# The samples' depthwise convolution moved from VectorE to GpSimd, and six prompt taps from TensorE to VectorE

## The reference

```python
def conv_mix(x, buf, w_pw1, b_pw1, w_dw, b_dw, ln_g, ln_b, w_pw2, b_pw2):
    h = x @ w_pw1 + b_pw1
    u = h[..., :D] * jax.nn.sigmoid(h[..., D:])
    full = jnp.concatenate([buf.astype(u.dtype), u], axis=1)      # 30 past rows, then the new ones
    c = depthwise_conv(full, w_dw, width=31) + b_dw               # one filter of 31 taps per channel
    cn = layernorm(c) * ln_g + ln_b
    out = jax.nn.silu(cn) @ w_pw2 + b_pw2
    return out, full[:, -30:]
...
def peer(x, w_q, sub_keys, u_tab, v_tab):                         # per token and head
    idx, gate = top 16 of the product keys, softmax
    act = gelu(sum_d u_tab[idx] * x)
    return sum_k gate_k * act_k * v_tab[idx_k]
```

## Time and profile before

| | |
|---|---|
| median of 3 runs | 3850.49 us (3847.3 to 3853.64) |
| the profiled execution's own time | 3850.32 us |
| its span, first to last instruction | 3848.5 us |
| mean granted clock of TensorE | 0.859 of full speed |
| busy: TensorE, VectorE, ScalarE, GpSimd | 74%, 71%, 38%, 37% of the span |
| gathers | 1152, with 1208 of 1313 MB moved |

### The profile page before, as it was taken

The page is one execution under the profiler, slowest core; times in us unless marked ns, Lnnn a source line. Parts: engine busy times, 40 slices in busy tenths (PEclk is TensorE's granted clock), DMA queues, the critical chain, the costliest instruction groups (busy, mean ns, idle before and its releaser), DMA issues.

```text
span 3848.5 us, 56215 instructions
## 1 busy us (share of the span) xinstructions
PE 2857.6 (74%) x20248; PEld 1343.3 (35%) x20248; DVE 2727.9 (71%) x6400; ACT 1449.0 (38%) x4376; POOL 1423.6 (37%) x1272
## 2 busy tenths in 40 slices
PE   7899998697666667788869657798786666666655
PEld 4667766442222212343324213344232222222211
DVE  5666665467666667777787767888776777777774
ACT  1333332134333334454444334444443333333333
POOL 0111111144444444444444444343344444444442
PEclk9999998897888878898889779999898877878777
DMA  2111110499999999999999999999999999999996
GB/s 79 36 31 27 43 31 18 159 426 426 427 426 426 427 427 426 418 388 402 408 426 422 426 425 426 389 383 373 397 416 426 426 425 427 427 426 426 425 426 283
DMA packets 230360, 1313.42 MB, mean 341 GB/s; under 512 B 58816, under 2 KB 62016, under 8 KB 82368
## 3 DMA queue, kind: packets, MB, share of 16 engines
q0 software_dynamic: 165888, 1208.03, 75.0%
q1 hardware_dynamic: 64192, 101.79, 7.5%
HBM read 1303.88 MB, written 5.86 MB: 340 GB/s over the span
## 4 chain that ended last, share of the span: by engine, by line
DMA 37%; PE 19%; DVE 18%; ACT 3%; issue 3%; DVEq 1%; ACTq 1%; POOL 1%; POOLq 0%
DMA arena<-in_uv,arena 37%; DVE arena L1780 9%; PE psum L1352 8%; PE psum L1314 4%; PE psum L1404 3%; PE psum L1434 2%; DVE arena L1869 1%; ACT wbuf L1570 1%; ACT arena L1565 1%; PE psum L1424 1%; DVE arena L1708 1%; POOL arena L1294 1%; DVE arena L1843 1%; DVE arena L1705 1%; DVE level L1732 0%
## 5 line engine op out<-in xcount | busy, mean ns | idle before, releaser
L1352 PE MATMUL psum<-arena,wbuf 64*64 64x512 f32 (+1 forms) x8704 | 1456.4, 743 | 864.5 <-ACT wbuf L1570 844.0
L1294 POOL DMA_INDIRECT arena<-in_uv,arena x1152 | 1344.2, 1167 | 1773.7 <-PE psum L1352 1571.7
L1780 DVE SCALAR_TENSOR_TENSOR arena<-arena 128x1024 f32<-128x1024 f32 x1152 | 1395.9, 1223 | 577.1 <-DMA arena<-in_uv,arena 550.4
L1352 PEld LDWEIGHTS psum<-arena,wbuf 64*64 64x64 f32 (+1 forms) x8704 | 336.1, 155 | 1759.9 <-ACT wbuf L1570 1364.1
L1561 ACT ACTIVATE arena<-arena 128x2 f32<-128x2 f32 x576 | 117.0, 203 | 1664.7 <-DVE arena L1780 1644.6
L1570 ACT ACTIVATE wbuf<-cst,arena 128x64 f32<-128x64 f32 x1152 | 338.1, 340 | 41.6 <-issue 2.4
L1314 PE MATMUL psum<-arena,wbuf 128*128 128x256 f32 (+1 forms) x1024 | 308.4, 449 | 8.4 <-DVE arena L1791 5.8
L1565 ACT ACTIVATE arena<-arena 128x1 f32<-128x1 f32 x1152 | 276.7, 287 | 41.5 <-issue 2.1
L1314 PEld LDWEIGHTS psum<-arena,wbuf 128*128 128x128 f32 x1024 | 201.6, 207 | 172.4 <-issue 130.7
L419 PE MATMUL psum<-arena,wbuf 128*128 128x288 f32 x672 | 189.0, 415 | 2.8 <-ACT arena L705 2.8
L1036 POOL COPY x<-arena 128x256 f32<-128x256 f32 x8 | 3.2, 397 | 423.2 <-DVE x L883 423.2
(11 more groups left out here) (273 smaller groups left out, 3155.4 us busy)
## 6 DMA issues: line engine op xcount, KB each, us to landing
wbuf<-in_w_q SPq DMA_DIRECT2D x64, 576.0 KB
arena<-in_w_pw SPq DMA_DIRECT2D x48, 512.0 KB
arena<-in_uv,arena POOLq DMA_INDIRECT x1152
wbuf<-in_w_rkv SPq DMA_DIRECT2D x24, 512.0 KB, 4.2
wbuf<-in_w_o SPq DMA_DIRECT2D x8, 512.0 KB, 3.7
arena<-in_w_o SPq DMA_DIRECT2D x8, 512.0 KB
x<-in_x SPq DMA_DIRECT2D x5, 576.0 KB, 6.1
arena<-in_state SPq DMA_DIRECT2D x16, 128.0 KB, 2.9
```

The source lines that it names most:

```text
L1294: pool.indirect_dma_start(ring[:, g % RING, :], None, I["uv"][p // 2], bass.IndirectOffsetOnAxis(ap=idx[:, s % 4, j:j + 1], axis=0)).then_ ...
L1352: last = pe.matmul(ps[e * HD:(e + 1) * HD, 2 * (u % 2) + a if u < NB else 4, :], diag[t, g % DIAGS, :], ring[t, g % RING, D + e * 512:D + ...
L1780: stt(out=row, in0=row, scalar=1.0, in1=tok[p % 2][:, UNITS[p % 2].index(u), :], op0=ALU.mult, op1=ALU.mult, accum_out=dots[:, g % COLS:g ...
```

## The change

The samples' convolution leaves VectorE and becomes a generator `samples` on GpSimd, run between its gathers. GpSimd's row is the one whose buffer its last gather took over, 11 rows behind that gather (`tick.now = g - RING - PHASE_ROW[2]`). VectorE's single reduction over 31 taps becomes additions in halves: 15 and 15, then 8, 4, 2, 1. Where one of these reads what the last one wrote, GpSimd waits for its own semaphore `sample_step`. `sampled` counts finished chunks; SP, VectorE and TensorE wait for it where they reuse or need what the samples' convolution reads or writes. In `cB` TensorE does 10 taps of the prompt and VectorE 21; `cA` stays at 16 and 15.

```diff
--- before.py
+++ after.py
@@ -1071,7 +1071,7 @@
 
 
     RING, DIAGS, LEAD, COLS = 11, 8, 2, 12
-    PE_TAPS = 16
+    PE_TAPS = (16, 10)
     HALFK = TOPK // 2
     UNITS, WIDTH, FROM = ((0, 1), (2, 3, 4)), (256, 320), (0, 256)
     PICKS = (TOPK, TOPK, TOPK, TOPK, HALFK)
@@ -1107,7 +1107,7 @@
     idx = R.cut(4, TOPK, dtype=U32)
     neg_max, gate, share, gate_sum, gate_inv = R.cut(4), R.cut(4, TOPK), R.cut(4, TOPK), R.cut(4), R.cut(4)
     dots, gelu, coef = R.cut(COLS), R.cut(COLS), R.cut(COLS)
-    tap_diags = R.cut(PE_TAPS, HD)
+    tap_diags = R.cut(max(PE_TAPS), HD)
     spare = R.cut(1)
     wb = [R.cut(C, P) for _ in range(2)]
     ups, uss = [R.cut(PAST + 2 * P) for _ in range(2)], [R.cut(SB, PAST + ST) for _ in range(2)]
@@ -1163,6 +1163,7 @@
             dve_names += [f"{n}.{x}{c}" for c in range(C) for x in ("glu", "tapped")]
             dve_names += each(n, "centred") + each(n, "scaled") + each(n, "into_x")
     pe_b, act_b, dve_b = Steps(K.sem("bg_pe"), pe_names), Steps(K.sem("bg_act"), act_names), Steps(K.sem("bg_dve"), dve_names)
+    sampled, sample_step = K.sem("conv_sampled"), K.sem("conv_sample_step")
     last_out = ("n0A", "n0B", "n1A", "n1B")
     ps = K.ps
     BANK = (5, 6)
@@ -1220,7 +1221,7 @@
                         sp.dma_start(wb[j], I["w_pw1"][2 * c + j]).then_inc(bl[j], 16)
                     if half:
                         if c >= 2:
-                            sp.wait_ge(dve_b.sem, dve_b.value(f"{n}.tapped{c - 2}"))
+                            sp.wait_ge(sampled, c - 1)
                             sp.wait_ge(stored, 32 * (c - 1))
                         sp.dma_start(uss[c % 2][:, :, 0:PAST], I["state_conv"][c]).then_inc(small[c % 2], 16)
                         if c:
@@ -1285,7 +1286,50 @@
 
         @block.gpsimd
         def _(pool):
+            tick = Tick()
+            HT = ST // 2
+
+            def samples(n, t):
+
+
+                summed = 0
+                for c in range(C):
+                    at = t["conv"] + c * t["chunk"] + 1
+                    us = uss[c % 2]
+                    weight = unsq(K.par[:, TAP0:TAP0 + TAPS, c], 1, SB)
+                    bias = K.par[:, B_DW, c:c + 1].unsqueeze(1).to_broadcast([P, HT, SB])
+                    yield from tick.until(at)
+                    pool.wait_ge(dve_b.sem, dve_b.value(f"{n}.glu{c}"))
+                    for e in range(2):
+                        out = cv[1][:, c, 2 * P:WIDTH[1]].rearrange("p (b t) -> p t b", t=ST)
+                        for i in range(HT):
+                            last = pool.tensor_tensor(prods[:, i], us[:, :, e * HT + i:e * HT + i + TAPS], weight, ALU.mult)
+                            if i < HT - 1:
+                                yield from tick.until(at + 4 * e + (i + 1) // 3)
+                        last.then_inc(sample_step, 1)
+                        summed += 1
+                        pool.wait_ge(sample_step, summed)
+                        for i in range(0, HT, 2):
+                            last = pool.tensor_tensor(prods[:, i:i + 2, :, 0:15], prods[:, i:i + 2, :, 0:15], prods[:, i:i + 2, :, 16:31], ALU.add)
+                        for m in (8, 4, 2, 1):
+                            last.then_inc(sample_step, 1)
+                            summed += 1
+                            yield from tick.until(at + 4 * e + (2 if m == 8 else 3))
+                            pool.wait_ge(sample_step, summed)
+                            last = pool.tensor_tensor(prods[:, :, :, 0:m], prods[:, :, :, 0:m], prods[:, :, :, m:2 * m], ALU.add)
+                        last.then_inc(sample_step, 1)
+                        summed += 1
+                        pool.wait_ge(sample_step, summed)
+                        last = pool.tensor_tensor(out[:, e * HT:(e + 1) * HT], prods[:, :, :, 0], bias, ALU.add)
+                        if e == 0:
+                            last.then_inc(sample_step, 1)
+                            summed += 1
+                            yield from tick.until(at + 4)
+                            pool.wait_ge(sample_step, summed)
+                    last.then_inc(sampled, 1)
+
             pool.memset(spare, 0.0).then_inc(row_done, RING)
+            work = samples("cB", times(2))
             for s, (p, head, u) in enumerate(SEQ):
                 pool.wait_ge(index_ready, s + 1)
                 for j in range(PICKS[u]):
@@ -1294,6 +1338,13 @@
                     pool.indirect_dma_start(ring[:, g % RING, :], None, I["uv"][p // 2],
                                             bass.IndirectOffsetOnAxis(ap=idx[:, s % 4, j:j + 1], axis=0)
                                             ).then_inc(here[g % RING], 16)
+                    if p == 2:
+                        tick.now = g - RING - PHASE_ROW[2]
+                        next(work, None)
+                if s + 1 == len(SEQ) or SEQ[s + 1][0] == 3:
+                    tick.now = 10 ** 6
+                    for _ in work:
+                        pass
 
         @block.tensor
         def _(pe):
@@ -1427,15 +1478,17 @@
                 def taps(c, at):
                     pe.wait_ge(act_b.sem, act_b.value(f"{n}.diags{c}"))
                     pe.wait_ge(dve_b.sem, dve_b.value(f"{n}.glu{c}"))
-                    for k in range(PE_TAPS):
+                    for k in range(PE_TAPS[half]):
                         yield from tick.until(at + k // 8)
                         for e in range(2):
                             q = slice(e * HD, e * HD + HD)
-                            last = pe.matmul(part[q], tap_diags[q, k, :], ups[c % 2][q, k:k + 2 * P], start=k == 0, stop=k == PE_TAPS - 1)
+                            last = pe.matmul(part[q], tap_diags[q, k, :], ups[c % 2][q, k:k + 2 * P], start=k == 0, stop=k == PE_TAPS[half] - 1)
                     last.then_inc(pe_b.at(f"{n}.tapped{c}"), 1)
 
                 def add_up(c):
                     pe.wait_ge(dve_b.sem, dve_b.value(f"{n}.tapped{c}"))
+                    if half:
+                        pe.wait_ge(sampled, c + 1)
                     return pe.matmul(total, K.ones, cv[half][:, c, :], start=c == 0, stop=c == C - 1)
 
                 yield from tick.until(t["project"])
@@ -1831,20 +1884,11 @@
                         dve.tensor_copy(up[:, 0:PAST], carry[:, c, :])
                         stt(out=up[:, PAST:], in0=ps[:, 5, 0:2 * P], in1=sg[:, 0:2 * P], **how)
                         dve.wait_ge(small[c % 2], 16 * (c // 2) + 16)
+                        if c >= 2:
+                            dve.wait_ge(sampled, c - 1)
                         stt(out=us[:, :, PAST:], in0=ps[:, 5, 2 * P:w].rearrange("p (b t) -> p b t", t=ST),
                             in1=sg[:, 2 * P:w].rearrange("p (b t) -> p b t", t=ST), **how).then_inc(dve_b.at(f"{n}.glu{c}"), 1)
                         dve.drain()
-
-                def sample_taps(c, us, e):
-
-                    weight = unsq(K.par[:, TAP0:TAP0 + TAPS, c], 1, SB)
-                    for i in range(ST // 2):
-                        at = e * (ST // 2) + i
-                        tt(prods[:, i], us[:, :, at:at + TAPS], weight, ALU.mult)
-                    dve.drain()
-                    out = cv[half][:, c, 2 * P:w].rearrange("p (b t) -> p t b", t=ST)[:, e * (ST // 2):(e + 1) * (ST // 2), :]
-                    dve.tensor_reduce(out=out, in_=prods, op=ALU.add, axis=AX.X)
-                    dve.drain()
 
                 if half == 0:
                     for up in ups:
@@ -1855,17 +1899,11 @@
                     yield from tick.until(at)
                     glu(c, up, us)
                     out = cv[half][:, c, 0:2 * P]
-                    if half:
-                        for e in range(2):
-                            yield from tick.until(at + 1 + 2 * e)
-                            sample_taps(c, us, e)
-                        rest = cv[half][:, c, 2 * P:w]
-                        ts(rest, rest, K.par[:, B_DW, c:c + 1], None, ALU.add)
                     yield from tick.until(at + 5)
                     dve.wait_ge(act_b.sem, act_b.value(f"{n}.tap_sum{c}"))
                     spread = t["chunk"] - 6
-                    for k in range(PE_TAPS, TAPS):
-                        yield from tick.until(at + 5 + (k - PE_TAPS) * spread // (TAPS - PE_TAPS))
+                    for k in range(PE_TAPS[half], TAPS):
+                        yield from tick.until(at + 5 + (k - PE_TAPS[half]) * spread // (TAPS - PE_TAPS[half]))
                         last = stt(out=out, in0=up[:, k:k + 2 * P], scalar=K.par[:, TAP0 + k, c:c + 1], in1=out, op0=ALU.mult, op1=ALU.add)
                         if k < TAPS - 1:
                             dve.drain()
```

## The result

The changed kernel takes 3899.3 us (3897.9 to 3901.2, 4 runs), the kernel before 3851.8 in the same comparison: a ratio of 1.0125, 95% interval 1.0111 to 1.0139. That is +47.5 us where 3870, some +20, was forecast. The sign was right, but the size was forecast at less than half. The time lies 0.7 us inside the upper end of the range (3838 to 3900), and that is luck: the range reached so far only for the rival in which GpSimd is the bound, which is not what happened.

What follows compares the result with a forecast made beforehand. VectorE was taken to bound the sample half's convolution, DMA close behind. From 3850.3 us, minus 32.6 net VectorE work, plus 47 collision, plus 5 late gathers, gives 3870 us; range 3838 to 3900.

Steps and rivals of the forecast that it cites:

- the rival in which GpSimd is the bound: Sample half's convolution: dear products and full waits make GpSimd need 360 to 384 us; 3885 to 3908 us, chance 0.15.
- The bound: Sample half's convolution, 325.8 us: VectorE, busy 289.5 us, is the tighter resource, with the DMA engines close behind.
- the DMA floor: Same stretch: even a free VectorE gains only about 7 us before the DMA engines bind, 31 at 426 GB/s.
- What is removed and added: VectorE in the convolution: 58.4 us of sample work removed, 25.8 us of prompt taps added, net 32.6 us less.
- So I leave it: VectorE's 11.4 us wait for the tap sum, left unchanged although VectorE arrives 7 us earlier in each chunk.
- GpSimd's own time: The 176 operations moved to GpSimd in the convolution take 98 us, between 80 and 128.
- The collision: Convolution: GpSimd's operations and VectorE's two-input SBUF instructions exclude each other, costing VectorE 47 us, ends 27 and 80.
- the 0.71: Share of VectorE's time in which dots and taps hold its two inputs, 207 of 293 us; scales the collision.
- The gathers behind it: Gathers queued behind GpSimd's products come late, mostly covered by the ring of 11 rows: 5 us for the stretch.
- The other waits: Waits for the gate product, SP's conv state load, sample reuse and TensorE's column sum were each put at 0.
- The faster rival: The two engines seldom meet in the convolution and the DMA engines bind: 3830 to 3843 us, chance 0.25.
- The signs named beforehand: Convolution of the changed kernel: expected instruction lengths, GpSimd's busy time, row waits and stretch length, all else as before.

Runs made afterwards that it cites:

- the taps alone: Kernel before with only TensorE's prompt taps cut to 10 and VectorE's raised to 21 in the sample half's convolution, samples still on VectorE: 3869.0 us, ratio 1.0048.
- 16 taps on TensorE: Changed kernel with the taps back at 16 on TensorE and 15 on VectorE, only the samples on GpSimd: 3878.6 us, ratio 1.0072.
- steps between them: Changed kernel with a semaphore wait between all of GpSimd's 22 operations of a chunk, so that no two stand back to back: 3879.5 us, ratio 1.0071.
- the memsets: Changed kernel with each of GpSimd's 22 operations a chunk replaced by a memset of like length that reads nothing from SBUF: 3843.2 us, ratio 0.9983.

## Why the prediction was right in sign and wrong in size

- **The bound.** Half right. That added VectorE work costs its full price is shown (the taps alone, +19). That removed work comes back is not: less work on VectorE brings almost nothing, more costs in full, for behind VectorE's own work stand its chain through TensorE and ScalarE for the tap sum (at once: 8 us less work is 10 us more waiting) and a floor 6 us below, at which the DMA engines are full. The prediction named the DMA floor (7 us below; measured 7.7) but not the chain.
- **What is removed and added.** Right: 56 us of instructions gone, 48 taps at 0.48 us each. "So I leave it", said of the wait for the tap sum, was a step that failed: it was weighed that VectorE comes earlier, and the wait was still left at 11.4 us. It measured 22.9, and 39.6 with 16 taps on TensorE. That is 11.5 us of the miss; the wait for the gate fell by 4.2 us against it.
- **GpSimd's own time.** A little low: 98 us were forecast, and the shortest of each kind give 64 x 0.824 + 32 x 0.701 + 16 x (0.774 + 0.478 + 0.377 + 0.264 + 0.253) = 110 us.
- **The collision.** The mechanism was right and the size wrong: 47 us forecast, 69 measured on taps and dots, 70 with the experts' numbers. This is the step that failed most: the price was taken from L933, where the two engines took turns. The changed kernel's strided products don't give VectorE a turn when they follow one another; it stands behind all three. With steps between them the loss is 44 us, next to the forecast 47, though no run tests the 0.71 and the prices in that sum one by one. The blocks are 25 us, the larger part of the miss. The rule of a lock held for one instruction ("SBUF — State Buffer", section "SBUF: two separate sides", in the Trainium skill) did not help: it gives the pair of ports to whichever side starts first and doesn't say who is next, and by the starts in this trace VectorE started first in 7 of the 13 worst cases and was held all the same.
- **The gathers behind it.** Right: waits for rows grew by 4.8 us where 5 were put, and the memsets show that the queue itself costs 1 us.
- **The other waits** at nothing: no wait for `sampled` or `sample_step` stands among those of 5 us or more on TensorE or VectorE.
- **The rivals.** The time lies in the band of "GpSimd becomes the bound", 3885 to 3908, but that isn't what happened: GpSimd waited 100 us for row counts, and with as long memsets the time is 3843. The faster rival could not have come true below 3842, the floor.
- **The signs named beforehand.** Means higher by "some 0.15 us" were higher by 0.25, single dots "near 1.8" were up to 4.1 us, GpSimd's products "averaging above 1" averaged 0.862, the stretch "340 to 350" was 378, GpSimd "near 300" was 262 us; waits for rows and all outside the stretch came as said.

The two mis-sized terms, 69 for 47 (+22) and the tap sum's wait (+11.5), make 33.5 us; the stretch's 52.2 and the forecast's -32.6 + 47 + 5 = 19.4 differ by 32.8. The wait for the gate (-4.2) and the 3.7 us of the balance that are in no term make up the difference.

## What to carry to other kernels

An elementwise operation moved from VectorE to GpSimd is no work taken off VectorE while its own instructions read two inputs from SBUF: here 56 us were moved and 69 came back. Before moving, count how much of VectorE's time in that stretch is two-input work. Let GpSimd read without a stride, or keep its strided reading instructions apart from one another: each was worth 20 to 25 us here, both together hardly more. Better still, let GpSimd do what reads nothing. And before freeing an engine that is busy 89% of a stretch, look for what it would wait for next: here a chain stood directly behind it and a floor 6 us below.

## What the runs showed of the hardware

- Three strided GpSimd products in a row stretched a VectorE tap of 0.48 us to 2.57, at the worst to 3.36, and a dot of 1.22 us to 4.13; with a semaphore wait between GpSimd's instructions the longest were 1.51 and 1.70 us. Beside products without a stride VectorE took turns (L933, 0.87 us twice) or mostly did (packed weights).
- A tap or dot that starts while GpSimd issues a gather can still be held by the product behind it: 0.35 us of lead did not help the tap of 2561.12 us. In the kernel before, where gathers follow one another, no dot took more than 1.297 us.
- Packed weights (a step of 4 and not 32 bytes) made a 128x248 product on GpSimd 0.663 us at its shortest instead of 0.824, and on VectorE 0.414 instead of 0.605. The step is dear on both engines. "GPSIMD Engine Reference", section "Performance pitfalls for Q7 kernels", in the Trainium skill, gives half as much again for each element; the trace has 1.24 times, for a whole instruction with two inputs.
- GpSimd's memset did not touch the two-input instructions. "SBUF — State Buffer", section "SBUF: two separate sides", in the Trainium skill, restricts that conflict to GpSimd operations that read SBUF; the runs agree, 1.223 us a dot beside 110 us of memsets.
- One one-input instruction did stretch beside two memsets, once: the scaling of the gates, 0.234 us in the median, took 0.806.
